# One transformer block on one core: attention values computed transposed from pre-scaled weights, and a late turn in the recurrent rounds

## Chip, core and metric

The kernel runs on 1 core of one Trainium2 chip. The metric is the device time of one execution in microseconds (us), the median of several runs. PE is TensorE, DVE VectorE, ACT ScalarE, POOL GpSimd, SP the engine that issues the loads.

## What is computed

Input x is 512 rows (tokens) of width 1024, everything in float32. Two layers follow each other. The first layer mixes tokens in two ways at once, over 8 heads of 64 columns each: a dilated attention and a recurrent scan (RWKV-7), whose outputs side by side go through `w_out`; a feed-forward part with a squared ReLU follows. The second layer is another attention with pooling and another feed-forward. The change touches the first attention and its place beside the recurrent scan:

```python
s = einsum(q, k) / sqrt(64), masked;  m = max(s);  p = exp(s - m)      # 3 branches, merged
num = sum(exp(m - m_all) * (p @ v));  den = sum(exp(m - m_all) * sum(p))
attn = rms_norm(num / den, attn_out_gain)         # over the 512 columns of the 8 heads
mixed = concatenate([attn, rwkv]) @ w_out
```

The kernel merges the three branches by adding the logarithm of how many of them see a key (`lncount`) to the score before the exponential.

## The kernel before

Matrix products with large weights are made as three products of fp32r parts (high by high, high by low, low by high: lines 499 to 501, 534 to 536, 625 to 627); the attention and the scan use plain float32 products. Every engine has one hand-written program and the engines meet at named semaphores.

**The stage of the change.** Between the input products and the output product of the first layer, PE runs one loop of four rounds (`i`, one for each block of 128 tokens of the scan) of five levels each (`l`, doubling steps of a triangular inverse). A level has two halves. In the even half PE issues `double` (line 815), the scores of the attention for the next query block (`scores`, line 926), a piece of the scan (`beside(i, 2l)`), and `attend(m)` for even m; then comes `update` (line 835, in the last level 837), and in the odd half another piece of the scan and `attend(m + 1)`. The next `double` waits for DVE's subtraction (line 2327) of what `update` gave and for a mask product on POOL (line 2619). `update` waits for two copies of what `double` gave, one on ACT (line 1664) and one on DVE (line 2320). m counts 32 (query block, head) items: pair p = m // 8 of heads, query block t = m // 2 % 4, head e = m % 2 of the pair; an item of query block t has t + 1 blocks of 128 keys. n = m // 2 counts the 16 (pair, query block) steps.

**One item of the attention.** DVE adds `lncount` to the scores in PSUM, writes them to Z1 and takes the minimum of the negated scores (`biased`, line 2253). ACT takes the exponential and the row sum (`weights`, line 1602). PE turns the weights, 128 by 128 at a time (`turn_weights`, line 935), ACT copies them to PT1 (`turned_weights`, line 1611), and PE multiplies with the values: the turned weights are the stationary operand of 128 columns, the 64 value columns of the head are streamed (`values`, line 945). When the four query blocks of a head pair are done, DVE scales them by the reciprocal of the row sums into On1 (`pair_output`, lines 2260 and 2262). After the last pair, ACT squares and sums the rows (`mix_norm`, line 1618), DVE scales the rows (line 2278), PE turns the result into the layout of the output product (`turn_mix`, line 954), and ACT copies it with the gain (`turned_mix`, line 1625). ACT rounds to the high part h_hi (line 1642), and DVE subtracts for the low part h_lo (`lower`, line 1817).

**The order on each in-order engine.** In `attend(m)` DVE does `biased(m + 2)`, ACT `turned_weights(m)` and then `weights(m + 2)`. PE's scores of step n wait until `biased` has emptied the two banks they go to (`max_ready`, 2n). In the first round ACT ends each level with one more activation (line 1670), which two POOL products wait for, and POOL's mask product for a later level is queued behind them.

**The pieces of the scan beside it** (PE; `beside`): half 0 `key_values` (800), 1 `solve` (848), 2 `carry` (858), 3 `receive` (866), 4 `grow` and `advance` (876 to 888), 5 `advance` and, from the third round, `turn_output` of the block two back (917), 6 `outputs` (898 to 909), 7 and 8 `gram` (765), 9 `turn_values` (773, 777); a round ends with `turn_keys` (784, 787). DVE has `received` in half 3 (2204, 2211), `advanced` in halves 4 and 5 (2218), `masked` in halves 7 and 8 (2190), the variance of a block's output in half 8 (2225) and its normalisation (`normalised`, 2235) in half 1 of the round after next, or in half 8 of the last round for the second last block; POOL takes the root in between (`root`, 2624). In half 9 of the last round PE turns the second last block (`turn_output`, 917). After the loop come the last `solve`, the first products with `w_out` (`out_first`, 534 to 536), the last block's steps between them, and the rest of the kernel.

```python
if n == 9 and i + 1 == NB:
    turn_output(i - 1, 7)          # PE waits for yn_ready, i.e. normalised
```

**Where the second attention differs.** It already uses the form that the change brings to the first: `scaled2` (lines 2379, 2381) multiplies each item's weights by the reciprocal of its row sum on DVE before they are turned, and `values2` (line 1098) holds 64 value columns stationary and streams the 128 turned weights of each head, the two heads of a pair into the two halves of the output partitions.

## Time and profile before

| what | value |
|---|---|
| median of 3 runs | 1293.64 us (1290.81 to 1295.12) |
| the profiled execution | 1293.62 us, its span 1291.9 us |
| PE busy | 1248.2 us, 97% of the span |
| DVE, ACT, POOL busy | 759.6, 582.2, 404.7 us (59%, 45%, 31%) |
| mean granted TensorE clock | 0.992 of full speed |

The span is from the first to the last instruction that the profile shows; the execution's own time is 1.7 us longer. Busy times of an engine overlap with those of others. An instruction listed in a timeline has its start and its duration; matmuls are pipelined, so the time that a group of them takes from PE's queue is the distance from its start to the next group's start, which is called its slot below. A float32 matmul shows as two records, a turn (a matmul with the identity) as one.

### The profile page before, as it was taken

Reading aid. Unit: us, or ns where it says so; the run is one execution under the profiler, and the core shown is the slowest. Engines: PE = TensorE matmul, PEld = TensorE weight load, DVE = VectorE, ACT = ScalarE, POOL = GpSimd, SP = SyncE. Lnnn points to the kernel's source line nnn. Section 1 sums busy time; section 2 is a strip of 40 time slices with the busy share of each in tenths; the row PEclk is TensorE's granted clock in tenths of the full one; section 3 lists DMA queues with packets and bytes.
Section 4 is the critical chain, followed back from the end, with each engine's and each line's share of the span. In section 5 each row is a group of like instructions: output and inputs, shape, how many; then the busy total and the mean of one; then the engine's idle time right before and its main releaser. Section 6 shows DMA issues by size and latency. Waiting matters only on the chain.

```text
span 1291.9 us, 26564 instructions
## 1 busy us (share of the span) xinstructions
PE 1248.2 (97%) x11253; PEld 1147.6 (89%) x11253; DVE 759.6 (59%) x1028; ACT 582.2 (45%) x1026; POOL 404.7 (31%) x314
## 2 busy tenths in 40 slices
PE   7999989999899999999999999999999999999997
PEld 7677787888799899999999997776798999999997
DVE  5579735455348726739558467434575395583763
ACT  5445525445335525526336353545444163361552
POOL 8022235233102525336235224000042362352520
PEclk9999989999899999999999999999999999999999
DMA  6223300000252232324332423210232233333331
GB/s 211 66 65 98 98 1 3 3 3 3 99 164 66 99 98 81 116 66 130 101 98 89 141 74 98 66 66 33 82 98 98 66 122 108 98 99 98 99 115 66
DMA packets 102073, 109.40 MB, mean 85 GB/s; under 512 B 1970, under 2 KB 97252, under 8 KB 101956
## 3 DMA queue, kind: packets, MB, share of 16 engines
q1 hardware_dynamic: 101876, 107.45, 26.3%
q8 instruction: 89, 1.46, 0.5%
q0 software_dynamic: 80, 0.26, 0.1%
q14 instruction: 28, 0.23, 0.1%
HBM read 105.60 MB, written 2.10 MB: 83 GB/s over the span
## 4 chain that ended last, share of the span: by engine, by line
PE 87%; DVE 6%; ACT 3%; DVEq 1%; issue 1%; POOL 0%; DMA 0%; ACTq 0%
PE ps L534 11%; PE ps L535 11%; PE ps L536 11%; PE ps L625 6%; PE ps L626 6%; PE ps L627 6%; PE ps L499 4%; PE ps L501 4%; PE ps L500 4%; PE ps L585 1%; DVE w_lo L1812 1%; PE ps L587 1%; PE ps L586 1%; ACT w_hi L1220 1%; PE ps L815 1%
## 5 line engine op out<-in xcount | busy, mean ns | idle before, releaser
L534 PE MATMUL ps<-w_hi,a_hi 128*128 128x256 f32 x1024 | 286.0, 279 | 0.0
L535 PE MATMUL ps<-w_lo,a_hi 128*128 128x256 f32 x1024 | 285.8, 279 | 0.0
L536 PE MATMUL ps<-w_hi,a_lo 128*128 128x256 f32 x1024 | 285.8, 279 | 0.0
L535 PEld LDWEIGHTS ps<-w_lo,a_hi 128*128 128x128 f32 x1024 | 192.4, 188 | 0.1
L534 PEld LDWEIGHTS ps<-w_hi,a_hi 128*128 128x128 f32 x1024 | 192.4, 188 | 0.1
L536 PEld LDWEIGHTS ps<-w_hi,a_lo 128*128 128x128 f32 x1024 | 192.4, 188 | 0.0
L1812 DVE TENSOR_TENSOR w_lo<-w_raw,w_hi 128x2048 fp32r<-128x2048 f32 (+1 forms) x57 | 136.8, 2400 | 85.6 <-ACT w_hi L1220 85.3
L1220 ACT ACTIVATE w_hi<-w_raw 128x2048 fp32r<-128x2048 f32 (+1 forms) x57 | 108.2, 1898 | 132.2 <-PE ps L536 107.5
L2690 POOL TENSOR_TENSOR hsq<-tmp 128x512 f32<-128x512 f32 x64 | 96.0, 1516 | 90.0 <-ACT tmp L1332 62.2
L1918 DVE TENSOR_TENSOR w_lo<-w_raw,w_hi 128x1024 fp32r<-128x1024 f32 (+1 forms) x72 | 95.1, 1335 | 26.5 <-ACT w_hi L1293 26.3
L625 PE MATMUL ps<-th,w_hi 128*128 128x256 f32 x384 | 108.1, 281 | 0.4 <-ACT tmp L1318 0.4
L626 PE MATMUL ps<-tl,w_hi 128*128 128x256 f32 x384 | 107.9, 281 | 0.0
L627 PE MATMUL ps<-th,w_lo 128*128 128x256 f32 x384 | 107.9, 281 | 0.0
L1293 ACT ACTIVATE w_hi<-w_raw 128x1024 fp32r<-128x1024 f32 (+1 forms) x72 | 54.7, 769 | 101.0 <-PE ps L536 91.9
L499 PE MATMUL ps<-h_hi,w_hi 128*128 128x512 f32 x224 | 93.0, 415 | 4.2 <-DVE w_lo L1812 3.9
L2666 POOL TENSOR_TENSOR hn_odd<-w_raw 128x512 f32<-128x512 f32 x24 | 31.2, 1300 | 186.2 <-DMA w_raw<-w_up_dram 62.9
L501 PE MATMUL ps<-h_hi,w_lo 128*128 128x512 f32 x224 | 88.6, 396 | 0.0
L500 PE MATMUL ps<-h_lo,w_hi 128*128 128x512 f32 x224 | 88.6, 395 | 0.0
L626 PE MATMUL ps<-h_lo,w_hi 128*128 128x256 f32 x288 | 80.9, 281 | 0.0
L625 PE MATMUL ps<-h_hi,w_hi 128*128 128x256 f32 x288 | 80.9, 281 | 0.0
L627 PE MATMUL ps<-h_hi,w_lo 128*128 128x256 f32 x288 | 80.9, 281 | 0.0
L1959 DVE TENSOR_TENSOR a_lo<-hsq,a_hi 128x512 fp32r<-128x512 f32 x64 | 62.2, 989 | 26.8 <-POOL hsq L2690 14.6
(379 smaller groups left out, 3104.7 us busy)
## 6 DMA issues: line engine op xcount, KB each, us to landing
w_raw<-w_ffn_up_dram SPq DMA_DIRECT2D x16, 1024.0 KB, 5.6
w_raw<-w_ffn_down_dram SPq DMA_DIRECT2D x16, 1024.0 KB, 5.1
w_raw<-w_up_dram SPq DMA_DIRECT2D x16, 1024.0 KB, 5.7
w_raw<-w_down_dram SPq DMA_DIRECT2D x16, 1024.0 KB, 5.2
w_raw<-w_in_first_dram SPq DMA_DIRECT2D x12, 1024.0 KB, 5.3
w_raw<-w_out_dram SPq DMA_DIRECT2D x8, 1024.0 KB, 5.1
xn<-x_dram SPq DMA_DIRECT2D x8, 512.0 KB, 5.7
w_raw<-w_in_dram SPq DMA_DIRECT2D x4, 1024.0 KB, 5.5
```

The source lines that it names most:

```text
L499: mm(o, whi, hi[:, hb + k, :], start=first and k == 0, stop=False)
L500: mm(o, whi, lo[:, hb + k, :], start=False, stop=False)
L501: m = mm(o, wlo, hi[:, hb + k, :], start=False, stop=last and k == KT - 1)
L534: mm(o, hi[:, hb + k, tok], whi, start=first and own and k == ks[0], stop=False, skip_group_check=True)
L535: mm(o, hi[:, hb + k, tok], wlo, start=False, stop=False, skip_group_check=True)
L536: m = mm(o, lo[:, hb + k, tok], whi, start=False, stop=last and k == ks[-1], skip_group_check=True)
L625: mm(o, whi, hi[:, k, :], start=begin and k == 0, stop=False, skip_group_check=True)
L626: mm(o, whi, lo[:, k, :], start=False, stop=False, skip_group_check=True)
L627: m = mm(o, wlo, hi[:, k, :], start=False, stop=k == KH - 1, skip_group_check=True)
L1220: af(w_hi[:, g % 2, :, 0:n], w_raw[:, g % 2, :, 0:n], ACT.Copy).then_inc(sm["w_hi_ready"], 1)
L1812: v.tensor_tensor(w_lo[:, g % 2, :, 0:n], w_raw[:, g % 2, :, 0:n], w_hi[:, g % 2, :, 0:n].bitcast(F32), ALU.subtract).then_inc(sm["w_lo_re ...
L2690: g_.tensor_tensor(hsq[:, j, :], x, x, ALU.mult).then_inc(sm["square_f32"], 1)
```

## The change

In the first attention each item's weights are now scaled by the reciprocal of their row sum on DVE (`scaled1`, one reciprocal and one product for each of the 32 items) before they are turned. The values are stationary, the turned weights streamed, and both heads of a step are done together, in the even half of the next level, ahead of that half's `turn_weights`. The output comes out in the layout of the output product. ACT takes squares and a gained copy from PSUM once for each pair (`pair_output`); PE sums the squares over the 512 columns with three products by a matrix of ones (`mix_sum`); ACT takes the root; DVE takes reciprocals over 128x512 in two parts (m = 35, 36) and multiplies four tiles (m = 37, 38); ACT rounds in items 38 and 39, DVE takes the low parts in item 39. `mix_norm`, `turn_mix`, `turned_mix` and On1 go. SP's second load of `w_out` waits for the last turned weights and no longer for the turned mix. In the last round the variance of the second last block is taken in half 7 (before: 8), its normalisation in half 9 (before: 8), and PE's turn of it and DVE's scaling that follows are behind the last `solve`, outside the loop.

The diff, shortened (indentation cut; lines that only rename a semaphore count are left out):

```diff
@@ -80,10 +80,10 @@
-rinv1 = r("rinv1", [P, H])
-osq1 = r("osq1", [P, H])
-r("w_hi_rest", [P, 2 * KT * GW - 2 * S - 10 * H])
-On1 = r("On1", [P, TT, 512])
+rinv1 = r("rinv1", [P, 4 * H])
+r("w_hi_rest", [P, 2 * KT * GW - 2 * S - 12 * H])
+PT1_odd = r("PT1_odd", [P, 2, S])
+osq1 = r("osq1", [P, 2, S])
@@ -429,7 +429,7 @@
-sp.wait_ge(sm["o_turned"], HP)
+sp.wait_ge(sm["p_turned"], 4 * H)
@@ -929,47 +929,46 @@
 def turn_weights(m):
...
-    pe.wait_ge(sm["p_ready"], m + 1)
+    pe.wait_ge(sm["w_scaled"], m + 1)
...
-def values(m):
-    p, t, e = m // 8, m // 2 % TT, m % 2
-    if m % 8 == 0:
+def values(n):
+    p, t = n // TT, n % TT
+    if t == 0:
...
-    pe.wait_ge(sm["pt_ready"], m + 1)
+    pe.wait_ge(sm["pt_ready"], 2 * n + 2)
...
-        k = mm(ps[:, 7, e * 256 + t * N:e * 256 + (t + 1) * N], PT1[:, m % 2, j * P:(j + 1) * P],
-               Vn[:, j, p * P + e * N:p * P + (e + 1) * N], start=j == 0, stop=j == t)
+        for e in range(2):
+            k = mm(ps[half[e], 7, t * P:(t + 1) * P], Vn[:, j, p * P + e * N:p * P + (e + 1) * N],
+                   (PT1, PT1_odd)[n % 2][:, e, j * P:(j + 1) * P], start=j == 0, stop=j == t)
...
-def turn_mix(c):
-    pe.wait_ge(sm["o_scaled"], TT)
-    after("mix_f32", c - 1)
-    for t in range(TT):
-        k = nc.tensor.transpose(ps[:, 4 + c % 2, t * P:(t + 1) * P], On1[:, t, c * P:(c + 1) * P], ident[:, :])
-    k.then_inc(sm["o_turned"], 1)
+def mix_sum():
+    pe.wait_ge(sm["max_ready"], 4 * H)
+    pe.wait_ge(sm["o_added"], 1)
+    pe.wait_ge(sm["o1_ready"], HP)
+    for c, x in enumerate((osq1[:, 0, :], osq1[:, 1, :], PT1[:, 0, :])):
+        k = mm(ps[:, 4, :], ones[:, :], x, start=c == 0, stop=c == 2)
+    k.then_inc(sm["o_sum"], 1)
...
 def attend(m):
...
+    if m and m % 2 == 0 and m <= 4 * H:
+        values(m // 2 - 1)
...
-    if 0 < m <= 4 * H:
-        values(m - 1)
-    if 35 <= m < 37:
-        turn_mix(2 * (m - 35))
-        turn_mix(2 * (m - 35) + 1)
+    if m == 33:
+        mix_sum()
...
 def out_first(u):
...
-    pe.wait_ge(sm["mix_f32"], HP)
-    pe.wait_ge(sm["o1_ready"], HP)
@@ -1017,8 +1016,6 @@
-    if n == 9 and i + 1 == NB:
-        turn_output(i - 1, 7)
@@ -1049,6 +1046,7 @@
+turn_output(NB - 2, 7)
@@ -1597,32 +1595,32 @@
-    at_ = m // 8 * 8 + e * TT + n % TT
...
-       accum_out=rowsum1[:, at_:at_ + 1]).then_inc(sm["p_ready"], 1)
+       accum_out=rowsum1[:, m:m + 1]).then_inc(sm["p_ready"], 1)
...
 def turned_weights(m):
...
-    w = (m // 2 % TT + 1) * P
+    n = m // 2
+    w = (n % TT + 1) * P
...
-    if m > 1:
-        act.wait_ge(sm["pv_done"], m - 1)
-    af(PT1[:, m % 2, 0:w], ps[:, 6, 0:w], ACT.Copy).then_inc(sm["pt_ready"], 1)
-def mix_norm():
-    act.wait_ge(sm["o1_ready"], HP)
-    act.wait_ge(sm["pv_done"], 4 * H)
-    for t in range(TT):
-        af(PT1[:, t % 2, :], On1[:, t, :], ACT.Square, accum_out=osq1[:, t:t + 1])
-        act.drain()
-    af(osq1[:, 0:TT], osq1[:, 0:TT], ACT.Sqrt, bias=eps[:, 0:1], scale=1.0 / 512).then_inc(sm["o_sd"], 1)
-def turned_mix(c):
-    act.wait_ge(sm["o_turned"], c + 1)
-    af(qkT[:, c, :], ps[:, 4 + c % 2, :], ACT.Copy, scale=cols("attn_out_gain", c)).then_inc(sm["mix_f32"], 1)
+    if n > 1:
+        act.wait_ge(sm["pv_done"], n - 1)
+    af((PT1, PT1_odd)[n % 2][:, m % 2, 0:w], ps[:, 6, 0:w], ACT.Copy).then_inc(sm["pt_ready"], 1)
+def pair_output(p):
+    act.wait_ge(sm["pv_done"], TT * (p + 1))
+    if p == 2:
+        act.wait_ge(sm["o_added"], 1)
+    af((osq1[:, 0, :], osq1[:, 1, :], osq1[:, 1, :], PT1[:, 0, :])[p], ps[:, 7, :], ACT.Square)
+    af(qkT[:, p, :], ps[:, 7, :], ACT.Copy, scale=cols("attn_out_gain", p)).then_inc(sm["o1_ready"], 1)
+def upper_mix(c):
+    act.wait_ge(sm["o_scaled"], c + 1)
+    act.wait_ge(sm["y_done"], NB - 1)
+    af(h_hi[:, c, :], qkT[:, c, :], ACT.Copy).then_inc(sm["hhi_ready"], 1)
...
 def attend(m):
@@ -1630,16 +1628,14 @@
-    if m == 33:
-        mix_norm()
-    if 35 <= m < 37:
-        turned_mix(2 * (m - 35))
-        turned_mix(2 * (m - 35) + 1)
-    if m == 37:
-        act.drain()
-        act.wait_ge(sm["y_done"], NB - 1)
-        for c in range(HP):
-            af(h_hi[:, c, :], qkT[:, c, :], ACT.Copy).then_inc(sm["hhi_ready"], 1)
+    if m and m % 8 == 0 and m <= 4 * H:
+        pair_output(m // 8 - 1)
+    if m == 34:
+        act.wait_ge(sm["o_sum"], 1)
+        af(PT1_odd[:, 0, :], ps[:, 4, :], ACT.Sqrt, bias=eps[:, 0:1], scale=1.0 / 512).then_inc(sm["o_sd"], 1)
+    if m in (38, 39):
+        upper_mix(2 * (m - 38))
+        upper_mix(2 * (m - 38) + 1)
...
 def beside(i, n):
@@ -1708,14 +1704,14 @@
-        act.wait_ge(sm["pv_done"], 4 * H + TT * (p + 1))
+        act.wait_ge(sm["pv_done"], 2 * H + TT * (p + 1))
...
-        act.wait_ge(sm["pv_done"], 4 * H + TT * (p + 1))
+        act.wait_ge(sm["pv_done"], 2 * H + TT * (p + 1))
...
@@ -2254,29 +2250,34 @@
-def pair_output(p):
-    dve.wait_ge(sm["pv_done"], 8 * p + 8)
-    v.reciprocal(rinv1[:, :], rowsum1[:, 8 * p:8 * p + 8])
+def scaled1(m):
+    n, e = m // 2, m % 2
+    w = (n % TT + 1) * P
+    dve.wait_ge(sm["p_ready"], m + 1)
+    v.reciprocal(rinv1[:, m:m + 1], rowsum1[:, m:m + 1])
...
-    v.tensor_tensor(On1[:, :, p * P:(p + 1) * P].rearrange("q t (e n) -> q e t n", e=2),
-                    ps[:, 7, :].rearrange("q (e t n) -> q e t n", e=2, n=N),
-                    rinv1[:, :].rearrange("q (e t) -> q e t", e=2).unsqueeze(3).broadcast_to([P, 2, TT, N]), ALU.mult)\
-        .then_inc(sm["o1_ready"], 1)
+    v.tensor_scalar(Z1[:, n % 2, e, 0:w], Z1[:, n % 2, e, 0:w], rinv1[:, m:m + 1], None, ALU.mult)\
+        .then_inc(sm["w_scaled"], 1)
...
 def attend(m):
...
+    if m + 1 < 4 * H:
+        scaled1(m + 1)
...
-    if m and m % 8 == 0 and m <= 4 * H:
-        pair_output(m // 8 - 1)
-    if m == 34:
+    if m == 20:
+        dve.wait_ge(sm["o1_ready"], 2)
+        v.tensor_tensor(osq1[:, 0, :], osq1[:, 0, :], osq1[:, 1, :], ALU.add).then_inc(sm["o_added"], 1)
+    if m in (35, 36):
...
-        v.reciprocal(osq1[:, 0:TT], osq1[:, 0:TT])
+        columns = slice((m - 35) * 2 * P, (m - 34) * 2 * P)
+        v.reciprocal(PT1_odd[:, 0, columns], PT1_odd[:, 0, columns])
+    if m in (37, 38):
...
-        for t in range(TT):
-            v.tensor_scalar(On1[:, t, :], On1[:, t, :], osq1[:, t:t + 1], None, ALU.mult).then_inc(sm["o_scaled"], 1)
-    if m == 38:
+        for c in range(2 * (m - 37), 2 * (m - 36)):
+            v.tensor_tensor(qkT[:, c, :], qkT[:, c, :], PT1_odd[:, 0, :], ALU.mult).then_inc(sm["o_scaled"], 1)
+    if m == 39:
@@ -2296,22 +2297,21 @@
-    if n == 8 and i:
+    if n == 8 - (i + 1 == NB) and i:
...
-    if n == 8 and i + 1 == NB:
+    if n == 9 and i + 1 == NB:
...
-    if n == 9 and i + 1 == NB:
-        scaled_output(i - 1, 7)
...
+scaled1(0)
...
 for i in range(NB):
@@ -2339,6 +2339,7 @@
+scaled_output(NB - 2, 7)
```

## Rows read from the trace of the kernel before

**Rows 1.** The page: busy time of each engine.

```profile
PE 1248.2 (97%) x11253; PEld 1147.6 (89%) x11253; DVE 759.6 (59%) x1028; ACT 582.2 (45%) x1026; POOL 404.7 (31%) x314
```

**Rows 2.** Windows: stretch, then busy us (instructions) of PE, PEld, DVE, ACT, POOL; PEclk.

```profile
250.00:300.00 50.00, 47.95 (x1024) 41.52 (x1025) 28.14 (x67) 21.86 (x58) 18.96 (x15) 1.00 0.01 3
```

**Rows 3.** Waits of PE in the loop, 185 to 350 us.

```profile
PE ps L926 <- DVE negmax L2253: 2.5, 4, 0.7
...
PE ps L917 <- DVE rstd L2235: 1.7, 1, 1.7
...
PE ps L815 <- POOL tmp L2619: 1.4, 1, 1.4
```

**Rows 4.** Timeline of PE (start us, us, operation): old form (L945), new form (L1098).

```profile
245.25 1.00 PE L945 MATMUL ps<-Vn,PT 128*128 128x64 f32 x8
246.18 1.15 PE L815 MATMUL ps<-hsq,tmp 64*64 64x64 f32 x32
...
835.78 0.44 PE L1098 MATMUL ps<-hsq,Vn 128*64 128x128 f32 x4
836.15 0.38 PE L534 MATMUL ps<-w_hi,h_hi 128*128 128x256 f32 x1
...
849.49 1.09 PE L1098 MATMUL ps<-hsq,Vn 128*64 128x128 f32 x16
850.51 0.50 PE L1130 MATMUL ps<-h_hi,w_hi 128*128 128x512 f32 x1
```

**Rows 5.** Timeline of PE, product by ones; then the group of turn_mix.

```profile
80.81 1.02 PE L727 MATMUL ps<-hsq,ones 128*128 128x512 f32 x2
81.27 0.80 PE L499 MATMUL ps<-h_hi,w_hi 128*128 128x512 f32 x1
...
L954 PE MATMUL ps<-ident,On 128*128 128x128 f32 x16 | 2.1, 276 | 0.0
```

**Rows 6.** Timeline of DVE: scaling one item of four key blocks, second attention.

```profile
878.56 0.16 DVE L2379 RECIPROCAL rinv<-rowsum 128x1 f32<-128x1 f32 x1
878.79 0.49 DVE L2381 TENSOR_SCALAR tmp<-tmp,rinv 128x512 f32<-128x512 f32 x1
879.20 0.28 DVE L2370 CUSTOM_DVE_ANT_0 tmp<-bias,ps 128x128 f32<-128x128 f32 x1
```

**Rows 7.** Timeline of PE and DVE around one wait of the scores.

```profile
234.64 1.09 PE L835 MATMUL ps<-hsq,Rm 64*64 64x64 f32 x30
...
235.84 0.69 DVE L2327 TENSOR_TENSOR hsq<-hsq,ps 128x512 f32<-128x512 f32 x1 [1.90 <-PE ps L835]
...
238.42 0.69 DVE L2253 CUSTOM_DVE_ANT_0 Z<-lncount,ps 128x512 f32<-128x512 f32 x1 [0.18 <-issue]
...
239.17 0.49 PE L926 MATMUL ps<-qkT 64*128 64x128 f32 x4 [0.75 <-DVE negmax L2253]
```

**Rows 8.** Source line 2140: duration ns min/median/max of a reciprocal.

```profile
L2140 DVE RECIPROCAL lora_up<-lora_up x4: 3353/3354/3355, 88.5 to 158.0; 128x512 f32<-128x512 f32 x4
```

**Rows 9.** Timeline of PE at the end of the last round.

```profile
327.61 1.15 PE L835 MATMUL ps<-hsq,Rm 64*64 64x64 f32 x32
329.65 1.15 PE L815 MATMUL ps<-hsq,tmp 64*64 64x64 f32 x32 [0.89 <-DVE hsq L2327]
331.78 1.15 PE L837 MATMUL ps<-Rm,hsq 64*64 64x64 f32 x32 [0.98 <-ACT hsq L1664]
334.62 1.12 PE L917 MATMUL ps<-ident,rstd 128*128 128x128 f32 x4 [1.70 <-DVE rstd L2235]
...
338.18 3.68 PE L848 MATMUL ps<-KG,Rm 64*64 64x128 f32 x32 [0.73 <-ACT btn L1560]
...
345.75 0.69 PE L858 MATMUL ps<-btn,tmp 64*64 64x64 f32 x32
```

**Rows 10.** Windows at the end of the last round; columns as in rows 2.

```profile
333.00:334.00 1.00, 0.00 (x0) 0.00 (x0) 0.12 (x1) 0.00 (x0) 0.84 (x1) 0.83 1.10 349
342.00:344.00 2.00, 2.00 (x10) 2.00 (x11) 0.02 (x1) 2.00 (x4) 0.00 (x0) 0.52 0.26 104
```

More of the change, by code:

```diff
@@ L231, in program @@
             "bias_built", "p_scaled", "s_done", "max_ready", "p_ready", "p_turned", "pt_ready",
-            "pv_done", "o1_ready", "o_sd", "o_scaled", "o_turned", "mix_f32", "window_ready", "pooled",
+            "pv_done", "w_scaled", "o1_ready", "o_added", "o_sum", "o_sd", "o_scaled", "mix_f32", "window_ready", "pooled",
             "wb_hi", "wb_lo", "half_hi", "half_lo", "d_hi", "s_sum", "u_ready", "c_added", "a_ready", "t_sum", "t_pool", "t_hi", "t_lo",
@@ L1091, in values2 @@
                     if 0 < p < 3:
-                        pe.wait_ge(sm["mix_f32"], HP + p)
+                        pe.wait_ge(sm["mix_f32"], p)
                     if p == 3:
@@ L1697, in turned_weights2 @@
                 act.wait_ge(sm["p_turned"], 4 * H + m + 1)
-                act.wait_ge(sm["pv_done"], 4 * H + m // 2)
+                act.wait_ge(sm["pv_done"], 2 * H + m // 2)
                 af(PT2[:, m % 2, 0:w], ps[:, 6, 0:w], ACT.Copy).then_inc(sm["pt_ready"], 1)
```

## The prediction, made before the change was run

> **What bounds the kernel now.** I read the page first: PE is busy for 97% of the span, DVE for 59% [rows 1]. So what takes time from PE's queue, or leaves PE waiting, is the time. Then the windows of the loop that the change touches: PE is busy 47.95 of 50 us, DVE 28.1 [rows 2], so even here PE looks like the bound with DVE half free. The waits of PE say where that is not so [rows 3]: in four of the levels the scores wait for DVE's `biased`, 2.5 us in all, once PE waits 1.4 us for POOL's mask product, and once 1.7 us for the normalised block that `turn_output` turns. Last, the timeline at the end of the loop [rows 9] and the granted clock there [rows 10]: PE waits 0.89, 0.98 and 1.70 us with one group of 1.1 us between, and then the clock is at half, 1.2 for 2.4 GHz. From the means of the two windows the fall was at 333.7 us ((1 - 0.83) / 0.5 = 0.34 us before 334) and the rise at 343.9 us; the last `solve` took 3.68 us in it.
>
> **The values on PE.** The old form takes 0.93 us for 8 records (245.25 to 246.18), 0.116 us each [rows 4]. The new form stands in the second attention: 0.37 us for 4 records and 1.02 us for 16, that is (1.02 - 0.37) / 12 = 0.054 us for one more record and 0.15 us for each group [rows 4]. There are 160 records in both (80 products of two records): old 160 x 0.116 = 18.6 us, new 160 x 0.054 + 16 x 0.15 = 11.1 us, 7.5 us less. The Trainium skill (TensorEngine Tiling, Key Properties) states that changing the tiling mode drains TensorE, and each new group changes it twice; the 0.15 us agrees. Without a drain, by the slope alone, those groups would give 2.4 us more.
>
> `turn_mix` goes, 16 turns, 2.1 us [rows 5]; three products by ones come, 0.46 us each (80.81 to 81.27) [rows 5], 1.4 us. PE's queue is 8.2 us shorter in all.
>
> **Where these 8.2 us lie.** Before, half of the values (head 0 of each step) stood in the odd half, between `update` and the next `double`, for 0.26, 0.5, 0.7 and 0.93 us with one to four key blocks. All values now stand in the even half. That half is about 0.1 us longer than before, the odd half shorter by the whole 0.26 to 0.93. But the odd half is the one in which PE waits for DVE: `double` can't start less than 2.04 us after `update` (327.61 to 329.65) [rows 9], of which `update` covers 1.08; and the scores can't start before `biased`.
>
> **DVE's queue.** Each of 32 items gets a reciprocal and a product on DVE. For four key blocks they take 0.64 us from the first to the next operation (878.56 to 879.20) [rows 6]; less by the product's length for fewer, 0.44, 0.50 and 0.57 us by the same view. That is 17 us in the loop, against 3.6 us of `pair_output` that go. It is not DVE's sum that counts but its place: `scaled1(m + 1)` stands ahead of `biased(m + 2)`, and behind that the scores. Level 6 shows it: update at 234.64, DVE's subtraction 1.2 us later, transpose, two pieces of the scan, `biased` at 238.42, scores at 239.17, 4.53 us after the update, 0.75 us of it a wait [rows 7]. With `scaled1` of four key blocks ahead this is 4.53 + 0.64 = 5.17 us; PE, relieved of 0.7 us of values, is ready at 2.04 + 1.08 = 3.12 us. The wait becomes 2.05 us, and the level is 0.64 us longer, not 0.7 shorter. In such a level all relief turns into wait.
>
> **Level by level.** I went through the 20 levels this way, each update against the same update of before; values behind a wait give nothing. Round 1: each of levels 0 to 3 has DVE's added scaling (0.50, 0.57, 0.64, 0.44 us) in a ring: later `biased`, later exponential on ACT, later activation L1670 behind it, later POOL products, later mask product, for which PE waits already [rows 3]. 2.15 us of scalings, less 0.5 us of PE's relief that is not lost: +1.6 us. Round 2: solve and `advance` halves are long enough on PE to keep 0.4 us of relief each, three scores waits lose 0.8, 0.6 and, at the keys (which wait for ACT's copies of the turned values, whatever PE saves), 0.1: +2.3 us at its end. Round 3 in the same way: +3.6 us. Then the attention's scores are over and the relief is kept: level 15 gives 0.93 back (+2.7). `mix_sum` stands where DVE's answer was waited for anyway: level 17 stays at +2.7. Level 18 has no second half of `turn_mix` (1.0 us) but waits for the scaled output, which is not later than before: +0.8.
>
> **The last levels.** A reciprocal over 128x512 took 3.354 us [rows 8], so each of the two halves is 1.68 us on DVE in levels 17 and 18; they fit beside `advance` and `outputs`. Before the last update DVE has, one after the other, subtraction, transpose, variance (0.8 us) and two products (1.2 us), and only then the copy that `update` needs: the update is at about 333.7, before 331.8 [rows 9]: +1.9, with a wait of 2.1 us on PE. Behind it PE turns the keys at once, the 1.70 us wait of `turn_output` being gone from there, but ACT has two roundings ahead of its two copies of the keys, so `solve` is at 337.2 us, before 338.18: -1.0. `turn_output` behind it waits for nothing. SP's earlier load of `w_out` hits no queue: its user, ACT's split, stands where it stood. The low parts on DVE end at 338.5, before `out_first` wants them.
>
> **The clock.** The waits between 329.5 and 337.2 (0.96, 2.1 and 1.5 us with short groups between) are at least those after which the clock fell before [rows 9, 10]. I take it that it falls again. If it falls behind the keys, `solve` takes 3.65, the turn 0.9, `out_first` 3.1 us: 345.1 where 345.75 was [rows 9]: -0.65. If it falls ahead of the last update, solve starts at 338.6 and the same point is at 346.4: +0.65. Bounds of this term: -3.5 us if it never falls (solve 1.84, the turn 0.44, `out_first` 2.8 at full clock: 342.3), +1.5 if it rises one step later.
>
> New is that the waits inside the rounds grow past 1.5 us: 1.9 us for POOL in level 1, 2.05 in level 6, 1.6, 1.4 and 1.7 in levels 8, 11 and 13, where the longest of scores and mask waits were 0.7 and 1.4 [rows 3] and the clock held. The only waits that the clock fell on reached 1.7 us. One fall in these rounds costs PE half of its length; the one known lasted 10.2 us, so between 0 (none, or all of it absorbed by waits for DVE, which doesn't slow down) and 5.1 us. I take 0.9 us, one short fall half absorbed, nearer to zero since behind it PE is kept busy.
>
> **Sum.** End of the loop and first `out_first`: 0 (middle of -0.65 and +0.65); fall inside the rounds +0.9. Behind that point the kernel's queues are the same, so it goes on to the end: 1293.6 + 0.9 = 1294.5 us. The profiled execution was at 1293.62, the median at 1293.64, so nothing is to be shifted.
>
> **Rivals.** *Relief kept.* If DVE's added operations pass mostly in its idle time (it has 22 of 50 us [rows 2]) and the scores wait no longer than before, 7.5 + 0.7 us come off, and `turn_output`'s 1.7 us with them; some of it stays lost to POOL in round 1. That gives 1285 us, 1283 to 1289. For it speaks the page's DVE share; against it the chain of rows 7, which is a sum of durations. Chance 0.22.
> *The clock falls in the rounds* (the other side). Mechanism: waits of 1.5 to 2 us for `biased` and for POOL let the clock fall, PE does the next stretch at half, and it comes again in the next round. It decides once a wait is over about 1.7 us. One as long as that of rows 10 costs 5.1 us, two short ones with the +0.65 about as much: 1298.7 us, 1297.6 to 1302. Chance 0.23.
> *The move does nothing.* PE may wait at `solve` for ACT's copies and DVE instead of at `turn_output`; that is in the sum, -1.0 us at solve for a wait of 1.7 us removed. Its price if wholly void is +1 us, inside my forecast.
>
> **Numbers.** A measurement of this kernel can tell about 0.3%, 3.9 us, from no change. The forecast case, DVE's chain in place of PE's, holds 1290 to 1297.5 and has 0.55. Faster by over 0.3% is the first rival, 0.22; slower the second, 0.23. The range for 8 in 10, over all cases, is 1286.5 to 1299.5.
>
> **What would show it.** Right: the waits of L926 for DVE's `biased` grow from 2.5 to about 9 us over nine or ten levels; a wait of about 2 us at level 6; the group of values falls to about 11 us of slots; the last `solve` at half clock within 1.5 us of 338; in the windows a clock below 1.00 at most once inside the rounds. Wrong: waits for `biased` under 4 us (relief kept), `solve` in 1.9 us (no fall at the end), or a clock of 0.5 in two or more stretches between 195 and 320 us (the slow case).

## The result, and the profile after

The changed kernel takes 1305.98 us (median; 1302.81 to 1308.84), the kernel before 1293.64: a ratio of 1.0096, interval 1.0075 to 1.0117. It is slower by some 12 us, outside the range of the prediction. Its profiled execution ran 1305.98 us with a span of 1304.3.

The page of the changed kernel, busy time of each engine; beside [rows 1], PE is busy for the same time in all, and the span is 12.4 us longer:

```profile
PE 1248.4 (96%) x11243; PEld 1139.2 (87%) x11243; DVE 785.3 (60%) x1086; ACT 581.8 (45%) x1022; POOL 405.9 (31%) x314
```

The waits of PE from 183 to 365 us in the changed kernel (what PE waited for: us in all, times, longest):

```profile
PE ps L926 <- DVE negmax L2249: 12.5, 9, 2.5
PE ps L784 <- ACT Vb L1546: 2.4, 3, 0.9
PE ps L815 <- POOL tmp L2620: 2.3, 2, 1.7
PE ps L837 <- issue: 2.2, 1, 2.2
```

The scores' wait for the row minima is five times that of [rows 3], in nine levels; 2.2 us are new ahead of the last update. Windows of PE (stretch, length, busy, instructions, PEclk) in which the granted clock is below 1:

```profile
204.00:207.00 3.00, 2.40 (x34) 0.67 0.00 0
207.00:210.00 3.00, 3.00 (x37) 0.76 0.00 0
261.00:264.00 3.00, 1.96 (x28) 0.85 0.00 0
264.00:267.00 3.00, 3.00 (x50) 0.59 0.00 0
297.00:300.00 3.00, 3.00 (x38) 0.53 0.00 0
300.00:303.00 3.00, 2.92 (x80) 0.90 0.00 0
```

Three times inside the rounds the clock was at its lower level, 1.2 for 2.4 GHz, for some 3.4 us; the kernel before had none there (both have one from 186 to 195 us, ahead of the rounds). By the means of these windows the falls began at 205.0, 263.1 and 297.2 us, each 0.3 to 1.1 us behind the end of a wait of PE (1.72 us to 204.6, 2.39 to 262.0, 1.85 to 296.9). The price of a fall is 3 us x (1 - PEclk) summed over its windows: 1.7, 1.7 and 1.7 us, 5.1 in all.

Where the time was lost shows when each update (L835, in the last level L837) starts against the same update of before, in us, from the timelines of PE. `first carry` is L858 behind the last solve:

| | end of round 1 (level 4) | round 2 (level 9) | round 3 (level 14) | last update | first carry |
|---|---|---|---|---|---|
| predicted | +1.6 | +2.3 | +3.6 | +1.9 | 0 |
| changed kernel | +3.2 | +7.5 | +13.8 | +14.0 | +12.2 |
| e1_order | -0.3 | -0.4 | -0.2 | 0.0 | -3.0 |
| e12_gate | +1.4 | +7.4 | +9.8 | +10.1 | +4.4 |

(e1_order and e12_gate are experiments below; their profiled executions entered the loop 0.7 and 1.9 us ahead of before, the changed kernel level with it. The 1.9 us are no merit of e12_gate: its clock did not fall at 186 us.)

All of the loss is there by the end of round 3. Level 8 shows how it comes about, in the timeline of the changed kernel (start us, us, engine, operation):

```profile
258.27 0.71 DVE L2329 STREAM_TRANSPOSE Rm<-hsq 128x512 f32<-128x512 f32 x1
258.91 1.25 DVE L2186 TENSOR_TENSOR LA<-ps,tri 128x512 f32<-128x512 f32 x2
260.08 0.14 DVE L2258 RECIPROCAL rinv<-rowsum 128x1 f32<-128x1 f32 x1
260.24 1.26 POOL L2611 TENSOR_TENSOR Rm<-LA,lmask 128x512 f32<-128x512 f32 x1 [17.40 <-DVE LA L2186]
260.30 1.34 DVE L2260 TENSOR_SCALAR Z<-Z,rinv 128x256 f32<-128x256 f32 x1
261.57 0.41 DVE L2249 CUSTOM_DVE_ANT_0 Z<-lncount,ps 128x256 f32<-128x256 f32 x1
261.64 1.27 POOL L2613 TENSOR_TENSOR Rm<-identc,Rm 128x512 f32<-128x512 f32 x1
...
262.04 0.92 PE L926 MATMUL ps<-qkT 64*128 64x384 f32 x4 [2.39 <-DVE negmax L2249]
```

The scaling of 128x256 takes 1.34 us, where the same operation takes 0.35 us elsewhere, and it ends (261.64) 0.14 us behind a product of POOL (261.50) that had begun 0.06 us ahead of it. All 32 scalings (duration ns min/median/max):

```profile
L2260 DVE TENSOR_SCALAR Z<-Z,rinv x32: 285/486/1414, 189.1 to 318.3; 128x128 f32<-128x128 f32 x8, 128x256 f32<-128x256 f32 x8, 128x384 f32<-128x384 f32 x8, 128x512 f32<-128x512 f32 x8
```

The masks that DVE has just made (L2186) are what POOL's product waits for, so both engines set out together: the order of the code makes this meeting in rounds 2 and 3 (scalings at 260.30 and 306.80 us). In round 1 the scaling began 0.13 us ahead of that product (222.96 and 223.09) and took 0.29 us. Other products of POOL hit other scalings. Against the shortest of its width (0.28, 0.35, 0.42 and 0.49 us), 15 of the 32 scalings are longer, by 9.6 us in all.

### The profile page after: what moved, and what is told of

Read it like the earlier page. It is cut to its first block, busy times and chain, and to the rows that moved or that the text cites. A ratio compares the mean times of both kernels' runs of the same rounds, so it can differ in the third digit from the quotient of the medians.

```text
span 1304.3 us, 26619 instructions
## 1 busy us (share of the span) xinstructions
PE 1248.4 (96%) x11243; PEld 1139.2 (87%) x11243; DVE 785.3 (60%) x1086; ACT 581.8 (45%) x1022; POOL 405.9 (31%) x314
## 4 chain that ended last, share of the span: by engine, by line
PE 85%; DVE 7%; ACT 4%; issue 2%; DVEq 2%; DMA 0%; POOL 0%; ACTq 0%
PE ps L534 11%; PE ps L536 10%; PE ps L535 10%; PE ps L625 6%; PE ps L626 6%; PE ps L627 6%; PE ps L499 4%; PE ps L501 4%; PE ps L500 4%; DVE w_lo L1808 1%; PE ps L585 1%; PE ps L587 1%; PE ps L586 1%; PE ps L835 1%; ACT w_hi L1218 1%
## 5 line engine op out<-in xcount | busy, mean ns | idle before, releaser
L1955 DVE TENSOR_TENSOR a_lo<-hsq,a_hi 128x512 fp32r<-128x512 f32 x64 | 62.2, 988 | 26.8 <-POOL hsq L2691 14.6
```

## The experiments

**Order alone.** DVE does the minima of the next level ahead of the scaling.

```diff
 def attend(m):
-    if m + 1 < 4 * H:
-        scaled1(m + 1)
     if m + 2 < 4 * H:
         biased(m + 2)
+    if m + 1 < 4 * H:
+        scaled1(m + 1)
```

> The changed kernel with one thing different: on DVE each item's scaling stands behind the next bias operation, not ahead of it. Nothing else moves, and nothing is left out. Theory D (the scaling ahead of the bias operation, for which the scores wait, costs the time, and the long waits let the clock fall): the waits of the scores fall from 12.5 us to under 5, the clock stays at full speed inside the four rounds, and the time is 1290 to 1296 us. Rival E (the end of the last round and the longer products by ones are the cost): the time stays at 1302 or more. Rival C (PE then waits for the scaling instead, at the turn of the weights): the waits move from the scores to the turns and the time is 1298 or more.

Measured: 1292.35 us (1288.70 to 1296.54), ratio 1.0005 (0.9985 to 1.0025). Two operations in another order are worth 13.6 us by the medians and 0.91%, 11.8 us, by the ratios: the whole loss. Waits in e1_order:

```profile
PE ps L926 <- DVE negmax L2249: 4.6, 6, 1.3
PE ps L815 <- POOL tmp L2620: 2.4, 2, 1.7
PE ps L837 <- issue: 2.2, 1, 2.2
```

The clock, over the whole stretch from 195 to 330 us, is 1.00 in this execution (e7_order_values and e8_order_var_sum below have the same order, and in their profiled executions it fell once, at 204 us, for 1.7 us):

```profile
195.00:330.00 135.00, 123.27 (x2702) 1.00 0.06 18
```

The 15.25 us between the first carries (357.97 and 342.72) have their parts in the traces: 7.9 us less wait for minima, 1.2 less for ACT's copy Vb, 5.1 of clock inside the rounds, 1.7 of clock at the end: 15.9 (the clock's share is an upper bound, since some of a fall passes in waits). The scalings themselves are stretched here nearly as much as in the changed kernel, 15 of 32 by 8.2 us in all: POOL still holds them up, but the minima no longer stand behind them. So the loss needs the place ahead of what PE waits for; how much of it that place would cost with no stretching at all, no run shows.

**Length.** The scaling over the first 64 columns only, so that the other weights stay unscaled.

```diff
-v.tensor_scalar(Z1[:, n % 2, e, 0:w], Z1[:, n % 2, e, 0:w], ...)
+v.tensor_scalar(Z1[:, n % 2, e, 0:64], Z1[:, n % 2, e, 0:64], ...)
```

> The changed kernel, but each item's scaling covers only its first 64 columns (of 128 to 512); the rest of the weights stays unscaled, so less of the computation is done on DVE. In the changed kernel 14 of the 32 scalings take 0.6 to 1.4 us where others of the same shape take 0.3 to 0.5, and they end when a POOL operation ends. Theory L (a scaling waits for a POOL operation that runs, whatever its own length): the long ones stay at 0.8 us or more though they do an eighth of the work, the waits of the scores fall by 2 us at most, and the time is 1301 us or more. Rival S (the length of the scalings is the cost): none is above 0.4 us, the waits fall by 5 us or more, and the time is under 1299 us.

Measured: 1308.04 us, ratio 1.0104 (1.0068 to 1.0140). Its scalings (duration ns min/median/max), then the timeline of one of them:

```profile
L2260 DVE TENSOR_SCALAR Z<-Z,rinv x32: 254/256/1249, 189.6 to 322.0; 128x64 f32<-128x64 f32 x32
```

```profile
297.86 1.26 POOL L2630 TENSOR_TENSOR krkv<-ysq,xn 128x512 f32<-128x512 f32 x1 [8.21 <-DVE ysq L2237]
297.93 1.25 DVE L2260 TENSOR_SCALAR Z<-Z,rinv 128x64 f32<-128x64 f32 x1
```

64 columns alone take 0.25 us, and beside POOL 1.25. The size of the operation plays no part in the long ones: with an eighth to a half of the work the waits for the minima are 11.1 us for 12.5, and the time is no shorter, as theory L had it.

**POOL held back.** The operations stay as they are; POOL starts two of its pieces only behind the scaling that they hit.

```diff
 if i > 1:
+    pool.wait_ge(sm["w_scaled"], min(2 * (nl * i + 2) + 3, 4 * H))
     shifted_output(i - 2)
 if i + 1 < NB:
+    pool.wait_ge(sm["w_scaled"], 2 * (nl * i + 3) + 3)
     first_inverse(i + 1)
```

> The changed kernel in its own order, and GpSimd waits for VectorE's scaling before two of its pieces: the first product of a round's inverse (behind the masks of half 7) and the addition of the shifted output (half 5). In the changed kernel both start some 0.06 us ahead of a scaling, which then takes 1.34 (level 8), 1.34 (level 12) and 1.41 us (level 13) where undisturbed ones of these widths take 0.35, 0.35 and 0.42. Nothing else differs; each operation is the same. Theory (the scaling waits for the end of a GpSimd operation that started first): these scalings take 0.35 to 0.50 us, the waits of the scores in these three levels get 0.9 to 1.0 us shorter each (2.39, 1.85 and 2.48 to about 1.4, 0.9 and 1.5), one or two of the falls of the clock go: 1301.5 us (1299 to 1303.5). Rival (GpSimd's later start makes its own products late, or these waits are filled by something else): the waits shrink but the time stays at 1304.5 to 1307 us. Rival 2 (GpSimd has nothing to do with it): scalings as long as before.

Measured: 1298.26 us (1294.46 to 1301.73), ratio 1.0047 (1.0031 to 1.0063), 7.7 us under the changed kernel by the medians, 6.3 by the ratios, and 0.7 below the range expected. Level 8 in e12_gate:

```profile
262.51 0.35 DVE L2260 TENSOR_SCALAR Z<-Z,rinv 128x256 f32<-128x256 f32 x1
262.78 0.41 DVE L2249 CUSTOM_DVE_ANT_0 Z<-lncount,ps 128x256 f32<-128x256 f32 x1
262.94 1.27 POOL L2611 TENSOR_TENSOR Rm<-LA,lmask 128x512 f32<-128x512 f32 x1 [21.98 <-DVE Z L2260]
...
263.26 0.92 PE L926 MATMUL ps<-qkT 64*128 64x384 f32 x4 [1.40 <-DVE negmax L2249]
```

The wait is 1.40 us for 2.39; in levels 12 and 13 it is 0.86 and 1.49 for 1.85 and 2.48. POOL's product starts some 0.5 us later behind the masks, and the scaling of 128x256 takes 0.35 us for 1.34: this shows directly that POOL's timing sets the length of DVE's scalings. In the profiled execution the clock falls twice inside the rounds, the second time at the 2.48 us wait of level 6, which this edit leaves alone, and then for long (windows from 240 to 252 us at 0.74, 0.50, 0.50, 0.55: 5.1 us). With 6.8 us this execution loses more to the clock in the rounds than the changed kernel's 5.1. What puts it 7.8 us ahead at the first carry is 1.9 us at the entry, the shorter waits (9.4 for 12.5 us for the minima, 1.5 for 2.4 for ACT's copy Vb), and a clock that does not fall at the end of the loop (its solve takes 1.96 us for 3.68).

**Another instruction for the scaling.**

```diff
-v.tensor_scalar(..., rinv1[:, m:m + 1], None, ALU.mult)
+v.tensor_tensor(..., rinv1[:, m:m + 1].broadcast_to([P, w]), ALU.mult)
```

> The changed kernel, in its own order, with the scaling of the weights written as a tensor_tensor product with the reciprocal broadcast along the row, in place of the tensor_scalar: the same values. Theory L (the long scalings wait for a port that VectorE's tensor_scalar in its two-port form shares with GpSimd; a tensor_tensor, which e6_order_var's rows show at 0.64 to 0.69 us for 128x512 with GpSimd running beside it, doesn't): each scaling takes 0.2 to 0.7 us by its width, none over 0.8 us; the waits for the minima fall from 24 us in total to 6 to 12 us, with fewer falls of the clock: 1298 us (1295 to 1302). Rival (the place of the scaling in VectorE's order costs the time, however long it takes, and the stretching is a small part): waits stay near the changed kernel's, 1304 to 1307 us.

Measured: 1313.66 us, ratio 1.0162 (1.0133 to 1.0192): neither theory, and the slowest of all. Its scalings, then the timeline of level 8:

```profile
L2260 DVE TENSOR_TENSOR Z<-Z,rinv x32: 291/693/1641, 189.6 to 324.2; 128x128 f32<-128x128 f32 x8, 128x256 f32<-128x256 f32 x8, 128x384 f32<-128x384 f32 x8, 128x512 f32<-128x512 f32 x8
```

```profile
264.26 1.26 POOL L2611 TENSOR_TENSOR Rm<-LA,lmask 128x512 f32<-128x512 f32 x1 [20.49 <-DVE LA L2186]
264.32 1.48 DVE L2260 TENSOR_TENSOR Z<-Z,rinv 128x256 f32<-128x256 f32 x1
```

The "24 us in total" of my expectation is not PE's wait for the minima, which was 12.5 us; here it is 13.5. My expectation rested on tensor_tensor rows in which one operand lay in PSUM. With both in SBUF it waits for POOL just as the tensor_scalar does, and its own work is longer on top (0.42 for 0.35 us at 128x256). The minima (L2249), which read one operand from PSUM, keep their 0.41 us for 128x256 beside POOL (261.57 in the changed kernel), and so does the reduction L2221 with its single input (0.67 us at 262.24, POOL busy to 262.91). That is what the Trainium skill (SBUF — State Buffer, Who interferes with whom) states: DVE and GpSimd share one pair of ports, which a two-port tensor_scalar or copy locks for its whole length, and on whose read side a DVE operation with two SBUF inputs meets a GpSimd one that reads SBUF; who comes second waits. The traces agree in all four of these cases.

**The price of the clock.** Ten transpositions of the identity ahead of the scores in five levels keep PE busy in its wait; bank 7's columns are overwritten by the values.

```diff
+if m // 2 in (7, 9, 12, 13, 14):
+    ...
+    for _ in range(10):
+        nc.tensor.transpose(ps[:, 7, q:q + P], ident[:, :], ident[:, :])
 if m // 2 + 1 < 2 * H:
     scores(m // 2 + 1)
```

> The changed kernel with ten transpositions of the identity added on TensorE ahead of the scores of five levels (those in which the changed kernel's wait for the row minima was longest or in which its clock fell), into columns of bank 7 that the next values product overwrites; nothing else differs. The waits for the scaling stay, but TensorE is busy for about 1.1 us of each at full clock. Theory C (the three falls of the granted clock between 205 and 301 us, some 3.1 us each, follow from the idle stretches in front of them, and cost about 1.5 us each): the falls go where the idle goes, the fillers cost nothing where they fit in a wait: 1301.5 us (1299.5 to 1303.5) against the changed kernel's 1306. Theory D (the clock falls for another reason, and the waits alone make the loss): 1306 to 1309 us, falls at about the same places.

Measured: 1301.45 us (1298.73 to 1304.02), ratio 1.0076 (1.0053 to 1.0098). PE has more to do and the kernel is not slower: 4.5 us faster by the medians, but 0.20%, 2.6 us, by the ratios, and the two intervals overlap, so a gain in time is not clear of noise. Over the whole loop the clock is at 1.00 and the wait for the minima at half:

```profile
183.00:339.00 156.00, 136.59 (x2888) 1.00 0.05 16
```

```profile
PE ps L926 <- DVE negmax L2255: 5.9, 9, 1.2
```

The second and third fall were behind waits that are filled here. Where these five waits are not filled or shortened (the changed kernel, e2_short, e3_values_only, e9_tt), two or three of them go with a fall in each profiled execution; here none does. The mean clocks of the runs agree: 0.988 to 0.996, against 0.985 to 0.989 in the changed kernel. That speaks for theory C. The first fall (205 us) is ahead of any filler, so its absence is this execution's luck, and so is that of the fall at 186 us, with which it entered the loop 2.0 us ahead.

**The two parts apart.** e3_values_only is the changed kernel with the last-round part undone (variance, scaled output and turn as before); e4_turn_only is the kernel before with that part alone:

```diff
+turn_output(NB - 2, 7)
-if n == 9 and i + 1 == NB:
-    turn_output(i - 1, 7)
...
-if n == 8 and i:
+if n == 8 - (i + 1 == NB) and i:
     variance(i - 1)
...
```

> The changed kernel with its last part undone: in the last round the variance, the normalisation, the turn of the second last block and the scaling stand where they stood before; the attention keeps its new form. My forecast took 1 us of gain for this part at the last solve, so the time is 1306 to 1308. Rival: its wait in front of the last update (2.2 us, DVE's variance and two products ahead of the copy) costs more than the turn gave back; then 1303 or less.

> The kernel before with only the last part of the change: variance one half earlier, normalisation one half later, the turn of the second last block behind the last solve. It takes the wait of 1.7 us at the turn away. Theory: the solve starts about 2 us earlier and the clock may not fall: 1289 to 1292.5 us. Rival: the wait only moves to the keys and the solve, same time within 1 us.

Measured: e3 1307.46 us, ratio 1.0108 (1.0081 to 1.0136); e4 1287.34 us (1285.05 to 1290.01), ratio 0.9964 (0.9949 to 0.9979). So the loss belongs to the values' part (e3 is in the range of its theory), and the last-round part is a gain of its own, 0.36% or 4.7 us, more than I expected. The timeline of PE in e4_turn_only:

```profile
332.89 1.15 PE L837 MATMUL ps<-Rm,hsq 64*64 64x64 f32 x32 [0.98 <-ACT hsq L1663]
333.97 0.66 PE L784 MATMUL ps<-ident,ktb 128*128 128x128 f32 x4
334.46 0.60 PE L787 MATMUL ps<-ident,btb 128*128 128x128 f32 x4
335.85 1.96 PE L848 MATMUL ps<-KG,Rm 64*64 64x128 f32 x32 [0.78 <-ACT btn L1559]
```

The 1.70 us wait of [rows 9] is gone and so is the fall of the clock behind it: the solve takes 1.96 us for 3.68. That is the case which I had put as the lower bound of the clock's term (-3.5 us).

**In the good order.** e7_order_values is e1_order with the last-round part undone; e6_order_var is e1_order with the variance back in half 8; e8_order_var_sum is e6_order_var with the products by ones in fp32r (the lower lines of the diff):

```diff
-if n == 8 - (i + 1 == NB) and i:
+if n == 8 and i:
-osq1 = r("osq1", [P, 2, S])
+osq1 = r("osq1", [P, 2, S], F32R)
```

> As e1_order, with the last-round part undone (variance in half 8, scaled output in half 9, turn ahead of the last level's end): the value form alone, in the good order. Theory A (the two parts' gains stand beside each other: e4_turn_only gained 5 us on the kernel before): this one loses that gain against e1_order, 1297 us (1295 to 1299). Theory B (the last-round part gives next to nothing once the level chain is already late at its end, as e3_values_only against the changed kernel, 1.5 us): 1293.9 us (1292.5 to 1295.5). In both the clock falls near 335 to 345 us for some 10 us.

> As e1_order (minima of the next level ahead of the scaling), and in the last round the variance goes back to half 8, behind VectorE's copy of the last q half, with the normalisation in half 9; the turn stays behind the solve. Theory (the last update's wait of 2.2 us is VectorE's copy queued behind the variance and two products): 0.9 us of it goes, the wait is about 1.3 us, 1291.4 us (1290 to 1292.6) against e1_order's 1292.35. Rival (the two products alone make the copy late, or the normalisation then delays the next thing by as much): 1292.3 us (1291.5 to 1293.5) and the wait stays over 1.9 us.

> As e6_order_var, and the three products of the squares by ones are fp32r products instead of fp32 (ones and squares rounded on writing): each one pass instead of two. Theory (the three products hold TensorE for 2.75 us of the level, not the 1.4 of the prediction, and that lies on its path): about 1.8 us less than e6_order_var, 1289.6 us (1288.3 to 1291). Rival (VectorE and ScalarE behind the sum, or the waits after it, take the time back): as e6_order_var, within 0.7 us.

| kernel | median us (lowest to highest) | ratio (interval) |
|---|---|---|
| e7_order_values | 1294.31 (1291.55 to 1296.89) | 1.0015 (1.0000 to 1.0031) |
| e6_order_var | 1289.93 (1287.15 to 1293.84) | 0.9994 (0.9979 to 1.0010) |
| e8_order_var_sum | 1288.46 (1285.50 to 1291.04) | 0.9969 (0.9955 to 0.9983) |

e7 came out as theory B had it: the value form by itself gains nothing even in the good order. Its time bears out the number of theory B; its mechanism was not tested. e6's last update waits 1.3 us for 2.2. Its median is 2.4 us under that of e1_order, its ratio 0.1% under, so I take no more from it than the wait. e8 is 1.5 us under e6 by the medians, 0.25% by the ratios, with intervals that just meet; its three products take 0.85 us for 2.75:

```profile
317.85 0.93 PE L959 MATMUL ps<-osq,ones 128*128 128x512 f32 x3
318.70 1.09 PE L818 MATMUL ps<-hsq,tmp 64*64 64x64 f32 x30
```

Two more edits on top of e8: ScalarE's second pair of roundings moved behind its copies of the turned keys (e10_late), and that with the tensor_tensor scaling (e11_late_tt).

> As e8_order_var_sum, and ScalarE's second pair of roundings of the mix (h_hi of heads pairs 2 and 3) is moved behind its copies of the turned keys, so that the last solve waits for no rounding. Theory: in e6_order_var the pair (1.23 us) ended just before the first of these copies, and the solve waited 1.73 us; about 1 us of it goes: 1287.5 us (1286 to 1289). Rival (the first output products then wait for the low parts, or e8's solve wasn't late): as e8_order_var_sum, 1288.5 us within 0.7.

> As e10_late, with the tensor_tensor form of the scaling as in e9_tt. Theory L: behind the minima the scaling has slack, so the port costs little on the path there; the waits for the minima (4.5 us) lose 1 to 2 us and GpSimd's own products, which wait for the same port, end sooner (TensorE's waits for them 2.4 us): 1286 us (1284 to 1287.8). Rival (nothing of it is on the path in that order): as e10_late, within 0.7 us; or slower by 1 us, since the tensor_tensor takes up to 0.2 us more than an undisturbed tensor_scalar.

Measured: 1288.15 us, ratio 0.9979 (0.9963 to 0.9994), and 1288.97 us, 0.9978 (0.9961 to 0.9994). Neither edit can be told from e8. The 1288.15 us of e10_late lie in the ranges of both its theory and its rival; the rival is right that e8's solve wasn't late, for it waited 0.73 us there as in e10_late, and not the 1.73 of e6. The 1288.97 us of e11_late_tt are outside its theory. With the minima first, even the stretched tensor_tensor costs nothing that shows, and the wait for POOL (2.8 us in e11) is no shorter. The best kernels are e4_turn_only and e8_order_var_sum, 0.4 and 0.3% under the kernel before, and can't be told apart.

## Why the prediction was wrong, and what of it was right

The case forecast (DVE's chain in place of PE's) is the right mechanism, but two of its terms and the clock's were mis-sized: DVE's scalings were taken at their length alone, with nothing for POOL; PE's relief was taken at twice its size; and one short fall of the clock was taken where three came. The slower rival had the right second mechanism and sign, but 1298.7 us for 1306.

- **Values on PE, -7.5 us: right for the values, but the turns beside them were put at nothing.** A group of 16 records takes 1.03 us of PE's queue in e1_order (311.41 to 312.44), 1.02 by [rows 4]; all groups of the values take 11.2 us of slots there for 19.6 before. But the same turns of the weights (L935) take 13.5 us for 10.0. The turns just ahead of the update of level 9, before and then in e1_order:

```profile
257.92 0.44 PE L935 MATMUL ps<-ident,Z 128*128 128x128 f32 x2
258.19 0.33 PE L945 MATMUL ps<-Vn,PT 128*128 128x64 f32 x2
258.45 1.15 PE L837 MATMUL ps<-Rm,hsq 64*64 64x64 f32 x32
```

```profile
257.34 0.44 PE L946 MATMUL ps<-PT,Vn 128*64 128x128 f32 x4
257.71 0.44 PE L935 MATMUL ps<-ident,Z 128*128 128x128 f32 x2
258.08 1.15 PE L837 MATMUL ps<-Rm,hsq 64*64 64x64 f32 x32
```

  The slot of the two turns is 0.37 us where a 64*64 group follows, and 0.27 where values of the same tile form (128*128) follow. Before, the values stood between; now each of the 32 groups of turns has a group of another tile form right behind it. I had charged that change to the new values groups alone. With the products by ones, PE's queue from the first update to the last is 4.1 us shorter in e1_order (123.2 us of slots for 127.3), not 8.2.
- **Products by ones, 0.46 us each: the term was mis-sized.** They take 2.75 us for the three, 0.92 each:

```profile
328.18 1.96 PE L956 MATMUL ps<-osq,ones 128*128 128x512 f32 x4
329.97 1.02 PE L956 MATMUL ps<-PT,ones 128*128 128x512 f32 x2
330.93 1.09 PE L815 MATMUL ps<-hsq,tmp 64*64 64x64 f32 x30
```

  A fp32 product is two records here. I had read from [rows 5] the distance to the next product's start, which overlaps it. "Level 17 stays at +2.7" fails by it: from level 16 to level 17 the update went from +13.8 to +14.9, 1.1 us.
- **DVE's queue, 0.64 us for the scaling of four key blocks: the step that failed.** "With `scaled1` of four key blocks ahead this is 4.53 + 0.64 = 5.17": it was 5.66 us (238.11 to 243.77), the scaling 1.09 us for 0.49. I took the durations from the second attention [rows 6] and did not ask what POOL does at that time in the loop, though the rows of POOL in the rounds were there to read and the Trainium skill has the rule (SBUF — State Buffer, Who interferes with whom). "Grow from 2.5 to about 9 us over nine or ten levels" was 12.5 over nine.
- **Level by level, +3.6 us at the end of round 3: +13.8.** In round 1 (+3.2 for +1.6) the excess is the clock's fall at 205 us; in rounds 2 and 3 it is stretched scalings, two falls and the smaller relief. By the slots, the 13.8 us are 12.5 us of longer waits (10.0 of them for the minima) and some 4.5 of clock, less 3.3 of relief by values and turns together, where the prediction's own prices give about 6. The wait for POOL's mask in level 1, put at 1.9 us, was 1.7.
- **"Then the attention's scores are over and the relief is kept": wrong.** Level 15 gave nothing back: the update went from +13.8 to +14.6, and in e1_order from -0.2 to +0.5. "In such a level all relief turns into wait" holds wider than I had it: e1_order, with the scalings out of the way of the minima, entered the loop 0.7 us ahead and is 0.2 to 0.4 us ahead at the ends of the three rounds. Up to the last update its 4.1 us of relief meet 4.8 us of added waits (13.0 for 8.3 us).
- **Last levels: mostly right.** Wait ahead of the last update 2.19 us, predicted 2.1; from there to the first carry the changed kernel gains 1.8 us, predicted 1.9 as the middle of two cases (1.25 for the one that came). The terms of that sum, 337.2 + 3.65 + 0.9 + 3.1, give 344.85 and not 345.1.

```profile
345.81 1.97 PE L837 MATMUL ps<-Rm,hsq 64*64 64x64 f32 x32 [2.19 <-issue]
347.71 1.11 PE L784 MATMUL ps<-ident,ktb 128*128 128x128 f32 x4
...
350.41 3.68 PE L848 MATMUL ps<-KG,Rm 64*64 64x128 f32 x32 [0.73 <-issue]
...
357.97 0.70 PE L858 MATMUL ps<-btn,tmp 64*64 64x64 f32 x32
```

  The clock falls again, as I took it, ahead of the last update. Long waits of PE go with it, but do not decide it: without a wait of 1.7 us or more before the keys (e4, e6, e8) the solve takes 1.96 or 1.97 us; with the 2.19 us one (the changed kernel, e1, e5) or one of 2.10 at the turn (e3, e7) it is at half clock; yet e12_gate has the 2.19 us wait and a solve of 1.96 us.
- **Clock inside the rounds, one short fall, +0.9 us: the second step that failed.** There were three, 5.1 us by the windows. The rival's "it decides once a wait is over about 1.7 us" was met by five waits for the minima, 1.78 to 2.48 us. Two of them and POOL's 1.7 us were followed by a fall; the two longest (2.48 us) were not.
- **"Relief kept", 1285 us, 0.22.** Its sign is within reach only with both parts in another order (e8: 1288.5).

What stays open: how much of the gain of e12_gate, over its ten runs, is shorter waits (3.1 us for the minima in the one profiled) and how much is falls that go with them; and why the same wait is followed by a fall in one execution and not in another. e6_order_var is 5.2 us ahead of the kernel before at the first carry (340.52 and 345.75) and 3.3 by the span; part of the rest is a fall of the clock (the windows from 348 to 354 us at 0.91 and 0.52, 1.7 us).

## What to carry to other kernels

Before an operation is put into an engine's queue, look at what the engine that shares its ports does at that moment: a 0.35 us tensor_scalar took 1.34 us, and what stood behind it in the queue was on the path. Put the work that another engine waits for ahead of the work that has slack, and count the time by the chain from one update to the next, not by busy shares; where the chain is the bound, relief of the busiest engine is worth nothing (4.1 us of it gave none here). When a group of products leaves TensorE's queue, look at what its neighbours then stand beside: here the turns became 3.5 us longer. Waits of 1.7 to 2.5 us on TensorE cost a second time where the clock falls behind them, so a change that adds such waits is dearer than their sum.

## What was not expected of the hardware

A wait added to an engine (e12_gate) made the kernel faster, by 7.7 us of the medians, and fifty useless turns added to another (e5_fill) did not make it slower. And the clock's falls differ where PE's waits and instructions are the same: the 2.48 us wait of level 6 brought a fall of 5.1 us in e12_gate and none in the changed kernel; and with the same instructions up to there the kernel before fell in front of 189 us, e5_fill did not. The window of the kernel before, then that of e5_fill:

```profile
186.00:189.00 3.00, 1.82 (x32) 0.65 0.00 0
```

```profile
186.00:189.00 3.00, 1.19 (x33) 1.00 0.00 0
```

It shows in the spread of every kernel: the twelve runs of e6_order_var go from 1287.15 us at a mean clock of 0.998 to 1293.84 us at 0.989. The 6.7 us between equal programs are as much as most of the edits compared here are worth.
